# Normalising x before it is turned, and sharing the first modulation products, in a two-block transformer kernel

## The reference

```
cond = silu(c)                                   # 1024 values
sh1, sc1, gt1, sh2, sc2, gt2 = split(cond @ w_ada + b_ada, 6)
h = x * rsqrt(mean(x*x, over features) + 1e-6) * g_mix * (1 + sc1) + sh1
proj = h @ w_in                                  # attention inputs, latents, gates
```

## Time and profile before

| what | value |
|---|---|
| runs | 784.83, 788.76, 1863.85 us |
| profiled execution | 789.89 us, span of the core 788.1 |
| TensorE busy | 747.6 us, 95% |
| VectorE busy | 557.2 us, 71% |
| ScalarE busy | 443.0 us, 56% |
| mean granted clock of TensorE | 0.982 of full speed |
| DMA | 148.25 MB, mean 188 GB/s |

### The profile page before, as it was taken

How to read it: one execution, slowest core, us unless ns; L and a number is a source line. 1 busy time by engine, 2 the same in 40 slices (tenths; PEclk the granted TensorE clock), 3 DMA queues, 4 the chain that set the end, 5 groups by cost and what they waited for, 6 DMA issues and landing times.

```text
span 788.1 us, 14679 instructions
## 1 busy us (share of the span) xinstructions
PE 747.6 (95%) x5306; PEld 686.6 (87%) x5306; DVE 557.2 (71%) x1078; ACT 443.0 (56%) x840; POOL 63.8 (8%) x94
## 2 busy tenths in 40 slices
PE   3699999999999999999999999979799999999997
PEld 3599897899999899999999998768698999999997
DVE  3976439898797766666666797557876877776773
ACT  5327456665745654554554766368764655555452
POOL 8001002000356000000000003000000000000000
PEclk9799999999999999999999999789999999999999
DMA  9977796988797475765766575422153776566531
GB/s 294 350 217 243 185 224 202 292 260 274 230 316 227 134 214 169 202 187 167 203 188 162 126 201 164 116 78 85 55 161 108 222 208 183 175 197 186 173 93 54
DMA packets 186934, 148.25 MB, mean 188 GB/s; under 512 B 13662, under 2 KB 171296, under 8 KB 186872
## 3 DMA queue, kind: packets, MB, share of 16 engines
q1 hardware_dynamic: 183008, 143.61, 61.6%
q10 hardware_dynamic: 2232, 3.03, 2.0%
q0 software_dynamic: 1648, 1.00, 0.6%
HBM read 146.29 MB, written 1.36 MB: 187 GB/s over the span
## 4 chain that ended last, share of the span: by engine, by line
PE 87%; ACT 5%; DVE 4%; issue 2%; DMA 1%; POOL 0%; ACTq 0%; DVEq 0%; POOLq 0%
PE ps L2181 19%; PE ps L1814 15%; PE ps L1815 15%; PE ps L1816 14%; PE ps L2183 10%; ACT w_hi L699 1%; DVE w_lo L1160 1%; PE ps L2268 1%; DMA arena<-in_x 1%; PE ps L2160 1%; PE ps L2051 1%; PE ps L1880 1%; PE ps L1862 1%; PE ps L2073 1%; PE ps L2038 1%
## 5 line engine op out<-in xcount | busy, mean ns | idle before, releaser
L1160 DVE TENSOR_TENSOR w_lo<-raw,w_hi 128x1024 fp32r<-128x1024 f32 (+3 forms) x223 | 270.3, 1235 | 74.0 <-ACT w_hi L699 72.5
L2181 PE MATMUL ps<-h,w_hi 128*128 128x512 f32 x672 | 239.3, 396 | 0.0
L699 ACT ACTIVATE w_hi<-raw 128x1024 fp32r<-128x1024 f32 (+3 forms) x223 | 226.3, 1039 | 20.2 <-PE ps L1816 7.1
L2183 PE MATMUL ps<-h,w_lo 128*128 128x256 f32 x672 | 189.5, 282 | 0.0
L2181 PEld LDWEIGHTS ps<-h,w_hi 128*128 128x128 f32 x672 | 126.3, 188 | 28.6
L1814 PE MATMUL ps<-h,w_hi 128*128 128x256 f32 (+1 forms) x440 | 127.3, 289 | 3.5 <-ACT bias L1056 1.7
L2183 PEld LDWEIGHTS ps<-h,w_lo 128*128 128x128 f32 x672 | 126.2, 188 | 0.0
L1815 PE MATMUL ps<-h,w_hi 128*128 128x256 f32 (+1 forms) x440 | 124.0, 282 | 0.0
L1816 PE MATMUL ps<-h,w_lo 128*128 128x256 f32 (+1 forms) x440 | 124.0, 282 | 0.0
L1814 PE MATMUL ps<-g_hi,w_hi 128*128 128x256 f32 x352 | 98.6, 280 | 0.4 <-DVE g_lo L1479 0.4
L1815 PE MATMUL ps<-g_lo,w_hi 128*128 128x256 f32 x352 | 98.4, 280 | 0.0
(11 more groups left out here) (356 smaller groups left out, 1112.7 us busy)
## 6 DMA issues: line engine op xcount, KB each, us to landing
raw<-in_w_in SPq DMA_DIRECT2D x53, 512.0 KB, 5.3
raw<-in_w_down SPq DMA_DIRECT2D x44, 512.0 KB, 4.3
raw<-in_w_gate_up SPq DMA_DIRECT2D x44, 512.0 KB, 4.1
raw<-in_w_ada SPq DMA_DIRECT2D x32, 512.0 KB, 4.7
raw<-in_w_gate SPq DMA_DIRECT2D x22, 512.0 KB, 4.0
raw<-in_w_up SPq DMA_DIRECT2D x22, 512.0 KB, 5.0
raw<-in_w_ada SPq DMA_DIRECT2D x32, 256.0 KB, 5.5
raw<-in_w_o SPq DMA_DIRECT2D x8, 512.0 KB, 5.0
```

Of the source, the lines that this page charges most:

```text
L699: A(w_hi[:, m % HL, 0:w], raw[:, n % RAW, 0:w], ACT.Copy).then_inc(hi_done, 1)
L1160: V.tensor_tensor(w_lo[:, m % HL, 0:w], raw[:, n % RAW, 0:w], w_hi[:, m % HL, 0:w].bitcast(f32), sub).then_inc(lo_done, 1)
L2181: T.matmul(bank[:, :], hi, h2[:, k, :, :].rearrange("p a b -> p (a b)"), start=(k == 0), stop=False, skip_group_check=True)
L2183: ins = T.matmul(bank[:, 0:SEQ], lo, h_hi[:, k, :], start=False, stop=(k == KC - 1), skip_group_check=True)
```

## The change

The row scale moves in front of the turning: ScalarE multiplies x by its reciprocal by token (`xh`, in the storage of the bias tile), and TensorE turns the normalised x as well, into PSUM banks 6 and 7, two column blocks at a time (`x_hat`). The raw x is still turned and kept in `xT`, for the residual; VectorE now copies half of it. h comes from PSUM in two ScalarE activations with scale and shift, one with a high-part result, one in float32 (`h_piece`); VectorE only subtracts (`low0`). `scaled`, `factor(0)` and the two `keep_awake` are gone. For pieces 1 to 4 the products k = 0 and 1 are made by ScalarE (`mod_start`). Two small activations load ScalarE's tables for Silu and Sqrt ahead of time. The load order becomes: piece 0, lat0, three panels of piece 1, lat1, the fourth, lat2, three of piece 2, lat3, the fourth, lat4, piece 3, lat5, half of piece 4, lat6, the other half, lat7, kr. The sums of each piece, the one-hot products and the transpose of the small vectors stand between dense panels.

```diff
-AHEAD_OF = ((), (0, 1), (2, 3), (4, 5), (6,), (7,))
+PIECE_BEHIND = ((-1, -1, -1, -1), (0, 0, 0, 1), (2, 2, 2, 3), (4, 4), (5, 6))
...
+        for i, k in enumerate(range(0, KC, kn)):
+            directs.append((PIECE_BEHIND[q][i], [(0, kn, 2 * w, at_, w, cols(I["w_ada"], g * D + a * P, w, k, kn))
                                               for at_, g in ((0, 1), (w, 0))]))
             mod_panels.append((q, k, kn, 2 * w))
-            mod_count.append(mod_count[-1] + kn)
-
-    for q in range(len(PIECES) + 1):
-        for k in AHEAD_OF[q]:
-            panel("lat%d" % k, [(0, 1, D, 0, D, cols(w_in, C_CQ, D, k, 1))])
-        if q < len(PIECES):
-            ada_piece(q)
+            mod_count.append(mod_count[-1] + kn - (2 if q and k == 0 else 0))
+
+    for q in range(len(PIECES)):
+        ada_piece(q)
+    for k in range(KC):
+        panel("lat%d" % k, [(0, 1, D, 0, D, cols(w_in, C_CQ, D, k, 1))])
...
+        xh = bias[:, 2:8, :].rearrange("p a b -> p (a b)")[:, 0:TT * D].rearrange("p (t d) -> p t d", d=D)
...
+        def xh_t(c, n=SEQ):
+
+            return ps[6 + (c // 2) % 2][:, SEQ * (c % 2):SEQ * (c % 2) + n]
...
+                        sp.wait_ge(*((mod_init, 2 * mod_panels[order[o]][0])
+                                     if order[o] < ADA_FIRST and mod_count[order[o] + 1] == mod_count[order[o]] else
+                                     (mod_step, mod_count[order[o] + 1]) if order[o] < ADA_FIRST else
...
+            act.wait_ge(s("const_ready"), 1)
+            line(A(warm, eps_c, ACT.Silu))
             act.wait_ge(s("va_t"), 1)
             line(A(va[:, :], ps[5][:, 0:VA_ROWS], ACT.Copy), "va_ready")
             line.settle()
             line(A(cond[:, :], va[:, 56:64], ACT.Silu), "cond_ready")
+            line(A(warm, eps_c, ACT.Sqrt))
 
             arrived(act, "in_x")
             for t in range(TT):
                 line(A(sq[:, 4 * t:4 * t + 4, :].rearrange("p a b -> p (a b)"), x_tm[:, t, :], ACT.Square,
                        accum_out=small[:, 68 + t:69 + t]))
-            act.wait_ge(s("const_ready"), 1)
             line.settle()
             line(A(rms, small[:, 68:70], ACT.Sqrt, scale=1.0 / D, bias=eps_c), "rms_ready")
-            for b in range(4):
+            act.wait_ge(s("inv_col"), 1)
+            for t in range(TT):
+                line(A(xh[:, t, :], x_tm[:, t, :], ACT.Copy, scale=inv[:, t:t + 1]), "x_copied")
+
+            def mod_start(q):
+
+                m = mods_of[q][0]
+                n, w = direct_of[m], mod_panels[m][3]
+                act.wait_ge(raw_in[n % RAW], raw_count[n])
+                act.wait_ge(s("cond_ready"), 1)
+                if q >= 2:
+                    act.wait_ge(s("mod_mm"), q - 1)
+                for k in range(2):
+                    A(mod_acc[:, q % 2, k, 0:w], raw[:, n % RAW, k * w:(k + 1) * w], ACT.Copy,
+                      scale=cond[:, k:k + 1]).then_inc(mod_init, 1)
+
+            def h_piece(q):
+
+                act.wait_ge(s("gs_ready"), q + 1)
+                for c in range(*PIECES[q]):
+                    act.wait_ge(s("x_t"), 4 + c // 2 + 1)
+                    for dst, name in ((h_hi[:, c, :], "h_hi"), (sq[:, c, :], "h_ready")):
+                        line(A(dst, xh_t(c), ACT.Identity, scale=gs[:, 0, c:c + 1], bias=mod[:, 0, c:c + 1]), name)
+
+            split.ahead(0 - AHEAD)
+            mod_start(1)
+            for b in (2, 3):
...
+            h_piece(0)
+            split.ahead(2 - AHEAD)
+            mod_start(2)
+            act.wait_ge(s("rows_mm"), 1)
+            line(A(bias[0:A_HEADS, 0, :], ps[6][0:A_HEADS, 0:FW], ACT.Copy), "frow_copied")
+            line(A(vb[:, :], ps[6][:, FW:FW + VB_ROWS], ACT.Copy), "vb_ready")
+            split.ahead(3 - AHEAD)
+            h_piece(1)
+            split.ahead(4 - AHEAD)
+            mod_start(3)
+            split.ahead(5 - AHEAD)
+            act.wait_ge(s("rows_mm"), 2)
+            line(A(bias[0:NSA_HEADS, 1, :], ps[7][0:NSA_HEADS, 0:FW], ACT.Copy), "frow_copied")
+            h_piece(2)
+            mod_start(4)
+            split.ahead(6 - AHEAD)
+            h_piece(3)
+            split.ahead(nth("kr") - AHEAD)
+            h_piece(4)
...
+                mine = [k for k in range(k0, k0 + kn) if q == 0 or k >= 2]
+                for i, k in enumerate(mine):
+                    j = k - k0
                     src, dst = raw[:, n % RAW, j * w:(j + 1) * w], mod_acc[:, q % 2, k % 2, 0:w]
                     if k < 2:
                         ins = V.tensor_scalar(dst, src, cond[:, k:k + 1], None, mult)
                     else:
-                        dve.wait_ge(mod_step, mod_count[m] + j - 1)
+                        if q and k < 4:
+                            dve.wait_ge(mod_init, 2 * (q - 1) + k - 1)
+                        else:
+                            dve.wait_ge(mod_step, mod_count[m] + i - 1)
...
-            def scaled(c):
-                line.settle()
-                line(stt(out=sq[:, c, :], in0=xT[:, c, :], scalar=gs[:, 0, c:c + 1], in1=NRM, op0=mult, op1=mult), "h_ready")
+                line(stt(out=gs[:, 0, a:b], in0=mod[:, 1, a:b], scalar=1.0, in1=va[:, 48 + a:48 + b], op0=add, op1=mult), "gs_ready")
 
             def low0(c):
                 dve.wait_ge(s("h_hi"), c + 1)
-                line.settle()
-                line(stt(out=h_lo[:, c, :], in0=sq[:, c, :], scalar=mod[:, 0, c:c + 1], in1=h_hi[:, c, :].bitcast(f32),
-                         op0=add, op1=sub), "h_lo")
+                dve.wait_ge(s("h_ready"), c + 1)
+                line(V.tensor_tensor(h_lo[:, c, :], sq[:, c, :], h_hi[:, c, :].bitcast(f32), sub), "h_lo")
...
+            for m in mods_of[0][0:3]:
+                mod_part(m)
+            inverse(0)
+            mod_part(mods_of[0][3])
+            for b in range(2):
+                dve.wait_ge(s("x_t"), b + 1)
+                line(V.tensor_copy(xT[:, 2 * b:2 * b + 2, :].rearrange("p a b -> p (a b)"), ps[b][:, :]))
+
+            split.ahead(0 - AHEAD)
+            gain_shift(0)
+            mod_part(mods_of[1][1])
+            low0(0)
+            mod_part(mods_of[1][2])
+            low0(1)
+            split.ahead(1 - AHEAD)
+            mod_part(mods_of[1][3])
+
+            split.ahead(2 - AHEAD)
+            mod_part(mods_of[2][1])
+            gain_shift(1)
+            mod_part(mods_of[2][2])
+            low0(2)
+            split.ahead(3 - AHEAD)
+            low0(3)
+            mod_part(mods_of[2][3])
+
+            split.ahead(4 - AHEAD)
+            mod_part(mods_of[3][0])
+            gain_shift(2)
+            mod_part(mods_of[3][1])
+            low0(4)
+            split.ahead(5 - AHEAD)
+            low0(5)
+
+            gain_shift(3)
+            mod_part(mods_of[4][0])
+            split.ahead(6 - AHEAD)
+            low0(6)
+            mod_part(mods_of[4][1])
+
+            split.ahead(nth("kr") - AHEAD)
+            gain_shift(4)
+            low0(7)
+            line.skip("h_ready", KC)
...
+            def x_hat(c0):
+
+                for c in (c0, c0 + 1):
+                    for t in range(TT):
+                        ins = T.transpose(xh_t(c)[:, t * P:(t + 1) * P], xh[:, t, c * P:(c + 1) * P], ident[:, :])
+                line(ins, "x_t")
+
             pe.wait_ge(s("const_ready"), 1)
+            pe.wait_ge(s("x_copied"), TT)
+            x_hat(0)
             mod_sums(0)
-            factor(0)
+            x_hat(2)
+            pe.wait_ge(s("x_copied"), TT + 2)
+            lat_panel(0)
             arrived(pe, "in_rel")
-            pe.wait_ge(s("x_copied"), 4)
-            T.matmul(ps[0][0:A_HEADS, 0:FW], relc[:, 0:A_HEADS], onehot[:, 0, :], start=True, stop=True).then_inc(s("frow_mm"), 1)
-            T.matmul(ps[1][0:NSA_HEADS, 0:FW], relc[:, A_HEADS:NB], onehot[:, 1, :], start=True, stop=True).then_inc(s("frow_mm"), 1)
             arrived(pe, "in_vb")
-            line(T.transpose(ps[2][:, 0:VB_ROWS], vb_rows[0:VB_ROWS], ident[0:VB_ROWS, 0:VB_ROWS]), "vb_t")
+            pe.wait_ge(s("h_lo"), 2)
+            T.matmul(ps[6][0:A_HEADS, 0:FW], relc[:, 0:A_HEADS], onehot[:, 0, :], start=True, stop=True)
+            line(T.transpose(ps[6][:, FW:FW + VB_ROWS], vb_rows[0:VB_ROWS], ident[0:VB_ROWS, 0:VB_ROWS]), "rows_mm")
+            mod_sums(1)
+            lat_panel(1)
+            lat_panel(2)
             pe.wait_ge(s("frow_copied"), 1)
             pe.wait_ge(s("vb_ready"), 1)
-            for q in range(1, len(PIECES)):
-                mod_sums(q)
-                for k in range(*PIECES[q - 1]):
-                    lat_panel(k)
-                if q <= 2:
-                    keep_awake(ps[6], 2)
-            lat_panel(KC - 1)
+            x_hat(4)
+            pe.wait_ge(s("h_lo"), 4)
+            line(T.matmul(ps[7][0:NSA_HEADS, 0:FW], relc[:, A_HEADS:NB], onehot[:, 1, :], start=True, stop=True), "rows_mm")
+            mod_sums(2)
+            lat_panel(3)
+            pe.wait_ge(s("frow_copied"), 2)
+            x_hat(6)
+            mod_sums(3)
```

(60 more changed lines are left out.)

10 lines of the change are left out of this document (4 added, 6 removed).

## The result

The changed kernel took 781.52 us (median of 8 runs, 779.74 to 785.19) against 786.02 for the kernel before (8 runs now). The ratio is 0.9936, 95% interval 0.9915 to 0.9957: 5.0 us less by the ratio, 4.5 by the medians. By the 2% mark that is no change; it is clear of noise all the same. One of the eight runs before, 1863.85, is a slow run and does not count in the ratio. The profiled execution took 780.94, its span 779.1.

What follows compares the result with a forecast made beforehand. TensorE bounds the kernel (busy 95%, 87% of the chain). +8.9 start, -1.7 -1.8 -1.6 work moved in, +1.7 keep-awake, +0.7 half clock, +0.4 before kr, -2.5 idle: net +4.1 off 788.76, so 784.7 us; range 779.3 to 790.

Steps and rivals of the forecast that it cites:

- the wait before lat2: TensorE idles 2.1 us before lat2, because h_piece(1) stands behind lat3's high part in ScalarE's order.
- Start of lat0: First dense panel on TensorE: starts at 22.6 instead of 31.48 us, 8.9 gained.
- From lat0 to kr: TensorE's stretch between these panels: 31.4 us of work plus idle time of 2.5, kr at 56.4.
- rival (b): Clock falls before lat0 in TensorE's idle stretches; a cost of 2.3 makes the gain 1.8, 787.0 us; chance 0.18.
- my own sign (0.50 in the clock between 17 and 40): Granted clock in the prologue: the forecast would be wrong if 0.50 stood between 17 and 40 us.
- The row at 561: Profile stretch at 561 us, cited against a clock fall: 1.6 idle of 2.0 us left the clock at 1.00.
- rival (c): lat3 lands a panel later (33.0): TensorE idles 3.6 before lat2, clock falls, 0.2 us gain left; chance 0.12.
- All releases of the six buffers come early enough: Panel loads in the prologue: buffers fall free in time for the forecast landings, up to lat3 at 31.5 us.
- The straight line of landings: Panel loads: 512 KB panels land in load order at 1.46 us each (359 GB/s), the queues being full.
- The tail from kr on: After kr, TensorE-bound work keeps its length: equal distance from kr to the end, 727.6 us.

Runs made afterwards that it cites:

- e5: The changed kernel run again unaltered; ratio 0.9951 to the kernel before.
- e6: The changed kernel with unread products filling three idle stretches of TensorE ahead of lat0; 783.55 us, ratio 0.9950 to the kernel before.
- e7: e6 with e1's order on ScalarE (h of pieces 1 and 2 ahead of the high parts of lat3 and lat5); ratio 0.9909 to the kernel before.
- e1: The changed kernel with ScalarE's h of pieces 1 and 2 put ahead of the high parts of lat3 and lat5; ratio 0.9910 to the kernel before.
- e9: The changed kernel with the load order of the kernel before, engines' orders unchanged; ratio 1.0021 to the kernel before.
- e11: e7 with the load order of the kernel before; ratio 1.0027 to the kernel before.
- e2: The changed kernel without the two small activations that load the Silu and Sqrt tables early; ratio 0.9946 to the kernel before.
- e3: The changed kernel with products k = 0 and 1 of pieces 1 to 4 back on VectorE; ratio 0.9889 to the kernel before.
- e4: The changed kernel with four products that nothing reads put between x_hat(2) and lat0; ratio 0.9889 to the kernel before.
- e8: The kernel before with only TensorE's sums of each piece moved behind the first dense panel of the piece before; ratio 1.0028 to the kernel before.

## Why the prediction was right

It was right in direction and size, and in the mechanism of the gain and of the wait before lat2. Its sum left out a cost of 1.6 for the clock; that it came out all the same is luck. 784.7 was forecast with 779.3 to 790, 781.52 was measured, against a base that is itself 2.7 lower on more runs (786.02 for 788.76). The forecast gain was 4.1; by kr it is 4.50 in the first trace and 3.77 in e5, by the medians 4.5.

- *Start of lat0*, forecast 22.6, was 21.92. The steps before it held to a few tenths: the root at 13.90 without a load (14.2 at its end), two rows of x to 17.1 (17.4), x_hat(0) at 17.22 (17.4), VectorE's PSUM copies 0.64 each (0.7), h at 0.45 between starts (0.45). Transposes were overestimated: four take 0.47 to 0.53, not 0.92. The price of 0.23 came from 16 transposes in 3.67, which is the half pace; at full pace e6 did them in 1.91. Of the 0.7, 0.4 is x_hat(0), 0.2 the sums (1.78 by starts, where I took the busy 2.02); x_hat(2) did not count, since TensorE waited 1.85 behind it. Another 0.8 came after lat0.
- *From lat0 to kr*, forecast 33.8, was 34.12. By starts: panels 24.6 (23.0), sums 5.15 (5.0), x_hat 0.96 (1.8), one-hot products and transpose 1.63 (1.6), waits 1.80 (2.5).
- *The panels' 1.6 too much is rival (b)*, which I gave 0.18, at a smaller price: 1.6 and not 2.3. By my own sign (0.50 in the clock between 17 and 40) the forecast's course was wrong there: 0.50 stood from 22.7 to 26.1. The evidence that I set against it was in part misread. I took the idle 1.27 before 16.64 for one that had left the clock up. But the 16 transposes before it took 3.67, where the 16 sums behind it, of the same size, took 2.02: the clock had been half, and came up in that idle time. The row at 561 stands, and so does one here: the wait of 1.80 before lat2, behind a full panel, left 1.00. The rule of the Trainium skill that I had set aside (TensorE: Matmul & The Clock Gate, "A second HAM failure mode: psum-queue depth-cycling": short idles between groups can bring the clock down) agrees with these traces in part: with waits of 1.84 and 1.85 before and behind the sums the clock fell, and with the stretches filled it stayed at 1.00 (e6, e7). The missing 0.7 at lat0's start, the cheap transposes (0.8 behind it) and 0.7 less waiting more than cancelled the 1.6.
- *The wait before lat2*, forecast 2.1 with ScalarE at lat3's load and h behind it: 1.80, lat3 awaited until 31.18 (31.5). e1 shows that it was that order. The mechanism of rival (c), a longer wait and a fallen clock behind it, is what e6, e9 and e11 ran into.
- *Wrong in it*: "All releases of the six buffers come early enough". e2, e3 and e4 show lat3's issue and landing moving with VectorE's position, and e9 what happens when they are late. The straight line of landings held for this one order because the order was made for it.
- *Not seen*: that most of the parts do little by themselves. The early table loads are worth about 0.4 by kr, the first products on ScalarE 0.8 at lat0 and about 0.6 at kr, the sums amid dense panels nothing alone (e8); the load order is needed for all of it (e9, e11).
- The tail from kr on kept its length but for the clock between 489 and 591, as expected of work that TensorE is bound by.

## What to carry to other kernels

When the first consumer starts nine microseconds sooner and the end moves by four, first take off the work that moved behind it (2.6 us here). For the rest look for the in-order queue where a late load stands in front of ready work: here ScalarE at one panel (1.6 us, two lines to swap), and SyncE's issue order (4 us when wrong). Load orders and engine orders must be changed together: the better of two orders depends on which buffer each engine frees first. Before a duration is taken as a price, compare it with the same work elsewhere in the trace: a transpose cost 0.23 us at the start and 0.12 later, for the clock. And where a change gives 0.5%, compare traces at a landmark behind the change; one profile's span had as much again from the clock elsewhere.
